# A fixed expert with 64 places, the lightest with 32, and small products moved inside a large one

## The reference

```
lg  = (xt @ w_rg).astype(float32) + b_rg;  grp = argmax(lg)      # one of 4 groups
le  = (xt @ w_re + b_re)[rows, grp]                              # its 4 experts
top_p, top_i = top_k(softmax(le), 2)                             # two experts a token
combine[token, expert] = softmax(lg)[grp] * top_p / sum(top_p)
for e in range(16):
    h = silu(xt @ w_gate[e]) * (xt @ w_up[e])                    # 1024 -> 512
    y = y + combine[:, e:e + 1] * (h @ w_down[e])                # 512 -> 1024
```

## Time and profile before

| | |
|---|---|
| median of 3 runs | 734.3 us (731.09 to 735.54) |
| profiled execution | 737.11 us, of which 735.4 us are its span |
| busy in the span | PE 691.0 us (94%), DVE 260.0, ACT 184.3, POOL 143.9 |
| DMA | 185.66 MB, mean 252 GB/s |
| start of the expert products | 447.6 us |
| last product of the last expert | ends at 717.0 us |

### The profile page before, as it was taken

The page is one execution under the profiler, slowest core; times in us unless marked ns, Lnnn a source line. Parts: engine busy times, 40 slices in busy tenths (PEclk is TensorE's granted clock), DMA queues, the critical chain, the costliest instruction groups (busy, mean ns, idle before and its releaser), DMA issues.

```text
span 735.4 us, 14789 instructions
## 1 busy us (share of the span) xinstructions
PE 691.0 (94%) x5461; PEld 443.2 (60%) x5461; DVE 260.0 (35%) x807; ACT 184.3 (25%) x459; POOL 143.9 (20%) x227
## 2 busy tenths in 40 slices
PE   4999999999997988998999999999999999999886
PEld 2476587848545464556555558965658675555442
DVE  4156310147344648754343653011121101111216
ACT  3110213112134864683332111000110010111104
POOL 0404007220242178300000201011111211111000
PEclk9999999999999899999999898999999999999999
DMA  9996138243578177403595248969999999999973
GB/s 343 369 317 206 46 130 285 64 166 115 191 239 320 35 197 197 148 1 117 209 423 210 73 172 303 391 219 391 360 396 408 385 369 383 367 365 394 378 286 131
DMA packets 56833, 185.66 MB, mean 252 GB/s; under 512 B 9182, under 2 KB 30975, under 8 KB 50738
## 3 DMA queue, kind: packets, MB, share of 16 engines
q1 hardware_dynamic: 44770, 152.54, 55.0%
q0 software_dynamic: 11984, 32.11, 14.3%
HBM read 172.97 MB, written 14.32 MB: 255 GB/s over the span
## 4 chain that ended last, share of the span: by engine, by line
PE 82%; DMA 8%; DVE 5%; ACT 3%; issue 1%; SPq 0%; DVEq 0%; ACTq 0%
PE ps L682 76%; DMA ring<-in_w_down_dram 6%; PE ps L929 2%; PE ps L1207 2%; DMA ring<-in_w_out_dram 1%; DMA ring<-in_w_in_dram 1%; PE ps L956 1%; PE ps L776 1%; ACT tabs L1595 1%; PE ps L832 0%; DVE tabs L1989 0%; DVE ugr L1965 0%; DVE vnr L2136 0%; DVE xr L2132 0%; PE ps L1074 0%
## 5 line engine op out<-in xcount | busy, mean ns | idle before, releaser
L682 PE MATMUL ps<-ring,xr 128*128 128x512 f32 (+3 forms) x640 | 138.8, 414 | 9.6 <-DMA ring<-in_w_in_dram 9.6
L682 PEld LDWEIGHTS ps<-ring,xr 128*128 128x128 f32 (+1 forms) x640 | 68.4, 151 | 72.2 <-issue 58.9
L682 PE MATMUL ps<-ring,work 128*32 128x128 f32 (+2 forms) x512 | 76.0, 381 | 2.2 <-DMA ring<-in_w_out_dram 1.6
L682 PE MATMUL ps<-ring,vnr 128*64 128x256 f32 (+1 forms) x1024 | 72.6, 328 | 0.0
L426 POOL DMA_DIRECT2D ring<-in_sel_pages_dram x96 | 51.5, 536 | 93.1 <-issue 57.0
L682 PEld LDWEIGHTS ps<-ring,vnr 128*64 128x64 f32 (+1 forms) x1024 | 49.4, 123 | 23.5 <-issue 6.6
L2464 DVE COPY vnr<-ps 128x256 f32<-128x256 f32 (+2 forms) x16 | 8.5, 533 | 150.8 <-PE ps L1207 150.8
L682 PE MATMUL ps<-ring,qT 128*32 128x256 f32 (+2 forms) x304 | 57.9, 506 | 3.3 <-DMA ring<-in_w_down_dram 2.6
L682 PE MATMUL ps<-ring 128*128 128x128 f32 (+1 forms) x512 | 59.6, 279 | 0.0
L2734 POOL DMA_INDIRECT x_rows<-kvn,qbd x14 | 20.7, 1480 | 198.6 <-DVE kvn L2510 67.2
L682 PEld LDWEIGHTS ps<-ring 128*128 128x128 f32 x512 | 58.8, 191 | 0.3 <-issue 0.2
(11 more groups left out here) (394 smaller groups left out, 830.3 us busy)
## 6 DMA issues: line engine op xcount, KB each, us to landing
ring<-in_w_gate_dram SPq DMA_DIRECT2D x11, 2048.0 KB, 20.4
ring<-in_w_up_dram SPq DMA_DIRECT2D x10, 2048.0 KB, 22.0
ring<-in_w_down_dram SPq DMA_DIRECT2D x10, 2048.0 KB, 26.1
xr<-in_w_gate_dram SPq DMA_DIRECT2D x5, 2048.0 KB, 24.2
tabs<-in_w_up_dram SPq DMA_DIRECT2D x5, 2048.0 KB, 26.4
ring<-in_cmp_pages_dram SPq DMA_DIRECT2D x64, 128.0 KB, 5.3
ring<-in_cmp_pages_dram POOLq DMA_DIRECT2D x64, 128.0 KB, 5.5
ring<-in_w_in_dram SPq DMA_DIRECT2D x3, 2048.0 KB, 9.3
```

What stands on the lines that cost most here:

```text
L682: return nc.tensor.matmul(out, lhsT, rhs, start=start, stop=stop)
```

## The change

Expert 0 gets 64 places instead of 128 and the light form of product, which the first place did not have before. Place 3 gets 32 places instead of 64 and now takes the lightest of the fourteen; it has a form of its own (`tiny_gate_up`, `tiny_turned`, `tiny_down`): four products side by side in quarters of the array. The other places keep their sizes.

The router products of the last two tiles and two of the table products run between the inner steps of the last output product, not ahead of it. The table of gate weights (`weights_in_slots`, and `placed_weights` on VectorE) is built behind the first expert's gate and up products; in its old place there are five products of `kept_warm` where there were four. Three of the four pieces of down 2 are issued ahead of gate 4, once the table of weights is there; only the fourth still waits for the second up product. VectorE's product of h for expert 1 now waits for expert 0's down product, since h of expert 0 lies in the same buffer. The last up load is issued in two halves, and the last up product starts on the first.

```
+TINY_CAP = 32
 FIXED = 2
-HEAVY = (E - FIXED) // 2
-FULL_AT = (6, 8)
-FULL = len(FULL_AT)
-PASSES = 1 + -(-(TOK - LIGHT_CAP) // CAP)
+CAPS = (64, 128, 96, 32, 96, 64, 128, 64, 128, 64, 96, 64, 96, 96, 64, 64)
+FULL, HEAVY, PLAIN = (sum(c >= least for c in CAPS[FIXED:]) for least in (CAP, MIDDLE_CAP, LIGHT_CAP))
+PASSES = 1 + -(-(TOK - TINY_CAP) // CAP)
...
+    by_size = np.argsort([-n for n in CAPS[FIXED:]], kind="stable")
+    c[:, C_SX + by_size] = np.arange(E - FIXED)
...
+        hT_tiny, sg_tiny, h_tiny = qf[:, 512:640], qf[:, 1536:1664], qf[:, 1792:1920]
...
-            return cap_of(n) == cap_of(n - 1)
+            return cap_of(n) == cap_of(n - 1) or {cap_of(n), cap_of(n - 1)} == {LIGHT_CAP, TINY_CAP}
...
+                if n == E - 1:
+                    load(up_slots[n % 3][:, 0:SLOT // 2], slab("w_up", e)[:, 0:SLOT // 2], "spare_in")
+                    load(up_slots[n % 3][:, SLOT // 2:SLOT], slab("w_up", e)[:, SLOT // 2:SLOT], "wu_in%d" % (n % 3))
+                    return
...
-                if n == FIXED:
-                    sp.wait_ge(sem("flag_ready"), 1)
-                    sp.wait_ge(sem("u_mm"), 2)
-                for f in range(FE):
+                for f in range(FE - 1 if n == FIXED else 0, FE):
+                    if n == FIXED:
+                        sp.wait_ge(sem("u_mm"), 2)
                     load(down_slots[2][f], slab("w_down", placed[n])[:, D * f:D * f + D], "wd_in2")
...
                     up_in_turn(placed[n], n)
+                    sp.wait_ge(sem("flag_ready"), 1)
+                    sp.wait_ge(sem("slots_ready"), 3)
+                    for f in range(FE - 1):
+                        load(down_slots[2][f], slab("w_down", placed[FIXED])[:, D * f:D * f + D], "wd_in2")
...
                     ins = mm(pb[4 + n][:, :], mixT[r % 2][:, k, :], wo[:, k, W * n:W * n + W], k == 0, k == KD - 1)
+                    if r == 4 and n == 1 and k == 1:
+                        router(2)
+                    elif r == 4 and n == 1 and k == 3:
+                        tokens_in_slots(0)
+                        tokens_in_slots(1)
+                    elif r == 4 and n == 1 and k == 5:
+                        router(3)
...
-            router(2)
-            tokens_in_slots(0)
-            tokens_in_slots(1)
-            router(3)
...
-            kept_warm(3)
+            kept_warm(5)
             te.wait_ge(sem("weights_ready"), 1)
-            weights_in_slots()
-            kept_warm(1)
...
-                if is_split(n - 1):
+                if n and is_split(n - 1):
                     te.wait_ge(sem("hl_ready"), split_before(n))
-                else:
+                elif n:
...
-                        up_in(n)
-                        weights = up_slots[n % 3]
+                        if n == E - 1:
+                            te.wait_ge(sem("spare_in"), 48)
+                        else:
+                            up_in(n)
+                        weights = up_slots[n % 3 if n else 1]
                     wv = weights.rearrange("p (k f) -> p k f", k=KD)
                     for k in range(KD):
+                        if n == E - 1 and bank == 3 and k == KD // 2:
+                            up_in(n)
                         for q in range(2):
...
+            def tiny_gate_up(n):
+
+                te.wait_ge(sem("xt_ready"), 2 * n + 2)
+                if is_split(n - 1):
+                    te.wait_ge(sem("hl_ready"), split_before(n))
+                else:
+                    te.wait_ge(sem("h_ready"), n)
+                for bank, done in ((2, "g_mm"), (3, "u_mm")):
+                    if bank == 2:
+                        te.wait_ge(sem("wg_in%d" % (n % 3)), 16 * (n // 3 + 1))
+                        weights = gate_slots[n % 3]
+                    else:
+                        up_in(n)
+                        weights = up_slots[n % 3]
+                    wv = weights.rearrange("p (k f) -> p k f", k=KD)
+                    for k in range(KD):
+                        for q in range(4):
+                            ins = mm(pb[bank][32 * q:32 * q + 32, 0:128], xeT[n % 2][:, k, 0:TINY_CAP],
+                                     wv[:, k, 128 * q:128 * q + 128], k == 0, k == KD - 1)
+                    ins.then_inc(sem(done), 1)
+
+            def tiny_turned(n):
+
+                te.wait_ge(sem("hl_ready"), split_before(n) + 1)
+                te.wait_ge(sem("y_out0"), n - 1)
+                te.wait_ge(sem("y_out1"), n - 1)
+                nc.tensor.transpose(pb[5 + 2 * (n % 2)][:, 0:P], h_tiny, ident).then_inc(sem("hl_turned"), 1)
+
+            def tiny_down(n):
+
+                te.wait_ge(sem("h_ready"), n + 1)
+                te.wait_ge(sem("wd_in%d" % (n % 3)), DOWN_LOADS[n % 3] * (n // 3 + 1))
+                wv = down_slots[n % 3]
+                for f in range(FE):
+                    for d in range(4):
+                        ins = mm(pb[4 + 2 * (n % 2)][32 * d:32 * d + TINY_CAP, 0:256], hT_tiny[:, 32 * f:32 * f + TINY_CAP],
+                                 wv[f][:, 256 * d:256 * d + 256], f == 0, f == FE - 1)
+                        if f == FE - 1 and d % 2:
+                            ins.then_inc(sem("y_mm"), 1)
+
             def turn_of(n):
 
...
             turn_of(1)
+            weights_in_slots()
+            light_turned(0)
             first_of(1)
...
+            def placed_weights():
+
                 dve.wait_ge(sem("slot_mm"), 2)
                 in_order(pb[7][:, 128:128 + E])
                 link(V.tensor_copy(slot_w[:, 0:FIXED], pb[7][:, 128:128 + FIXED]))
                 link(V.tensor_copy(slot_w[:, FIXED:E], in_place))
                 for q in range(4):
                     V.tensor_copy(slot_w_rest[32 * q:32 * q + 32, :], slot_w[64:96, 0:E])
+                    V.tensor_copy(slot_w_low[32 * q:32 * q + 32, :], slot_w[0:32, 0:E])
                 V.tensor_copy(slot_w_high[64:128, :], slot_w[0:64, 0:E]).then_inc(sem("slots_ready"), 1)
 
             def overflow_flag():
...
-                after(dve, "y_mm", 2 * n - 2)
+                after(dve, "y_mm", 2 if n == 1 else 2 * n - 2)
...
-                    dve.wait_ge(sem("slots_ready"), 3)
                 for n in range(E * b, E * b + E - 1):
                     rows_out(n + 1)
                     multiplied(n)
+                    if n == 0:
+                        placed_weights()
```

More of the change, by code:

```diff
@@ L61, with cap_of, is_tiny @@
 LIGHT_CAP = 64
+TINY_CAP = 32
 FIXED = 2
[L63 to L66 removed]
+CAPS = (64, 128, 96, 32, 96, 64, 128, 64, 128, 64, 96, 64, 96, 96, 64, 64)
+FULL, HEAVY, PLAIN = (sum(c >= least for c in CAPS[FIXED:]) for least in (CAP, MIDDLE_CAP, LIGHT_CAP))
+PASSES = 1 + -(-(TOK - TINY_CAP) // CAP)
 EPS = 1e-6
+def cap_of(n):
+    return CAPS[n] if n < E else CAP
 def is_light(n):
[L72 to L79 removed]
+    return cap_of(n) == LIGHT_CAP
+def is_tiny(n):
+    return cap_of(n) == TINY_CAP
 BIG = 1e30
@@ L162, in constants @@
     c[:, C_WB:C_WB + WIN] = np.where(dist <= WIN, slope[:, None] * dist, BIG)
-    at = np.arange(FIXED, E)
-    light = np.array([is_light(n) for n in at])
-    full = np.array([cap_of(n) == CAP for n in at])
-    middle = ~light & ~full
-    c[:, C_SX:C_SX + E - FIXED] = np.select([full, middle], [np.cumsum(full) - 1, FULL + np.cumsum(middle) - 1],
-                                            HEAVY + np.cumsum(light) - 1)
+    by_size = np.argsort([-n for n in CAPS[FIXED:]], kind="stable")
+    c[:, C_SX + by_size] = np.arange(E - FIXED)
     j = np.arange(SEQ)
@@ L1284, in light_turned @@
                 te.wait_ge(sem("hl_ready"), split_before(n) + 1)
-                te.wait_ge(sem("y_out0"), n - 1)
-                te.wait_ge(sem("y_out1"), n - 1)
+                after(te, "y_out0", n - 1)
+                after(te, "y_out1", n - 1)
                 for c in range(2):
@@ L1366, in first_of @@
             def first_of(n):
-                if is_light(n):
+                if is_tiny(n):
+                    tiny_gate_up(n)
+                elif is_light(n):
                     light_gate_up(n)
@@ L1375, in last_of @@
             def last_of(n):
-                if is_light(n):
+                if is_tiny(n):
+                    tiny_down(n)
+                elif is_light(n):
                     light_down(n)
@@ L1394, in _ @@
                 last_of(n - 1)
-                if is_light(n):
+                if is_tiny(n):
+                    tiny_turned(n)
+                elif is_light(n):
                     light_turned(n)
@@ L1780, in y_out @@
                 par = n % 2
+                if cap == TINY_CAP:
+                    for d in range(2):
+                        ins = A(ye[par][0:TINY_CAP, 256 * d:256 * d + 256], pb[4 + 2 * par][32 * d:32 * d + TINY_CAP, 0:256],
+                                ACT.Copy, scale=slot_w_low[32 * d:32 * d + TINY_CAP, n:n + 1])
+                    ins.then_inc(sem("y_out0"), 1)
+                    return
                 if cap == MIDDLE_CAP:
@@ L2434, in overflow_flag @@
```

(18 more changed lines are left out.)

18 lines of the change are left out of this document (11 added, 7 removed).

## The result

The changed kernel takes 724.69 us (median of 20 executions, 720.18 to 734.78) against 733.71 us for the kernel before (20 executions). The ratio is 0.9886, 95% interval 0.9864 to 0.9907: 8.4 us (6.8 to 10.0) or 1.1% faster by the ratio, 9.0 by the medians. The ratio is of fast runs alone: two of the twenty executions, of 732.0 and 734.8 us, were in the chip's slower state and count in the median only. The forecast was 725.8 us.

A forecast was written before the change was run, and what follows sets the result against it. The prediction took the stream of weight loads as the bound. Hole 7, front 1.3 and last up 0.2 sum to 8.5 us: 737.11 becomes 728.6 profiled, 725.8 against the median; the forecast's own range is 721 to 729.

The forecast's parts named there:

- What bounds: Mixture: the stream of weight loads sets the end; TensorE's savings after 500 us bring no load forward.
- The hole: Load stream, 480 to 500 us: 6.4 us without transfer close; stream comes forward 5.9 to 7.9, taken as 7.
- Gate 5's issue: SP's wait for gate 2's product: freed 6.7 us earlier, at 487.4, with 2.5 us to spare.
- The new wait: Ahead of gate 2: VectorE forms h of expert 1 only after down 0, costing 0.8 us.
- Gathers: POOL's gather for expert 5 lands at 521.1, TensorE wants it at about 521.9: it just fits.
- The front: Routing's end: mixed small products keep the clock, so the residual starts earlier; 1.4 us gained or 1.3 lost, taken as +1.3.
- The last up: Up 15 in halves: its product can end at 709.7, but hangs on the chain behind down 13; 0.2 us, at most 2.
- Place 3, early down 2, the moved table: Mixture's start: place 3 saves TensorE 3.4 and 1.8 us, not counted in the sum; SP's wait for the table costs nothing.
- In full: Rival, whole kernel: TensorE's time counts in full, 13.3 us gained, 721.0 us; chance 0.07.
- Given back: Rival: stream gains 5.9, front loses 1.3, half clock in the last chain takes 1.7; 2.9 us, 731.4; chance 0.22.
- Starved, at half clock: Rival, behind down 13's landing: TensorE waits for loads and runs at half clock to the end; 9.9 us slower, 744.2; chance 0.07.

The follow-up runs named there:

- place3_64: Changed kernel with 64 places at place 3 again instead of 32: 726.57 us, ratio 0.9900 to the kernel before.
- up_7_8: Changed kernel with the last eighth of the up loads of places 6 to 14 left out: 721.43 us, ratio 0.9839 to the kernel before.
- expert0_alone: Changed kernel with all undone but expert 0's 64 places and the later table of weights: 727.37 us, ratio 0.9916 to the kernel before.
- end_order: Changed kernel with sizes of places 3 and 13 swapped, expert 15's gate and up with their loads ahead of down 14: 724.70 us, ratio 0.9900.
- apart: Changed kernel with the router and table products again ahead of the last output product: 725.04 us, ratio 0.9894 to the kernel before.
- warm_mixed: Changed kernel with router(3) behind the last output product's fourth step, one warming product ahead of router(4) and one behind it: 723.42 us, ratio 0.9871.
- expert0_128: Changed kernel with expert 0 at 128 places in full form, its new wait gone, the weight table in its old place: 734.15 us, ratio 0.9997.

## Why the prediction was right

Its number was right within 1.1 us, and its main step with it; but smaller terms were off and cancelled, and that part is luck. Counted from the first transposes, the last up load landed 6.9 us earlier (256.3 us and not 263.1), its product ended 1.7 us closer behind it, and the tail was 0.3 shorter: the 8.9 us of the mixture stage. The forecast had 7 and 0.2 for these, and 1.3 for the front, which gave 0.2.

- **What bounds.** Right. The stream of loads, not TensorE, sets the end: place3_64 adds 5.1 us of products and costs nothing that can be told, up_7_8 takes loads away and gains 3 to 4 us. Not tried was the hole by itself: no run issues gate 5 late with TensorE's work as in the changed kernel.
- **The hole.** Forecast 7 (5.9 to 7.9). (Six loads at the 5.9 printed are 35.4 us and not 35.2; the rows give 5.87.) Up 3 to up 5 took 10.0 us less: the six loads went at 5.5 us each, faster than the 5.9 I had from two of them. Then 32 loads from up 5 (495.1) to the last half of up 15 (695.9) took 200.8 us, 6.28 each and not 6.20, 2.3 us back. Net 7.7, and 6.9 from the first transposes, as up 3 landed 0.8 us later behind them. The total was right because one rate was better than forecast and the other worse. Why the rate fell a little was not tried.
- **Gate 5's issue.** Forecast 6.7 us earlier than before. Taken from the first transposes it went from 49.2 to 37.4 us, 11.9 us. I had charged the half clock (1.95 of 3.9 us) to expert 0's products in both kernels; it did not lie there this time, and they took 7.13 us: 2 of the 5 us. The other 3 I had left out: expert 0's transposes and the wait behind them take 1.2 us and not 2.8, as they are of 64 rows and at full clock, and the 1.5 us that TensorE waited for VectorE ahead of expert 1's products are filled by the table of weights. The 2.5 us to spare were really 7.8 (issued at 477.05, the loads ahead of it landed by 484.8).
- **The new wait.** Forecast 0.8 us at gate 2, measured 1.12.
- **Gathers.** "It just fits" held for expert 5, whose rows landed 0.8 us before TensorE wanted them. Expert 6's came too late, and this short wait lies in the chain that ended last (PE in order, of the changed kernel):

```profile
522.32 1.09 PE L1216 MATMUL ps<-cst,ugr 128*128 128x128 f32 x8 [0.81 <-DMA ugr<-h_rows,qbd]
```

- **The front.** Forecast +1.3, measured 0.2 over that stage. The step that failed is "I take +1.3, as the long run of small products is broken up": the product did keep the clock in this execution (whether for the mixing is open, see expert0_alone) and `residual(4, 1)` did come 1.8 us earlier, limited by `chosen_of(3)` as forecast, but the half clock then fell on the products behind it.
- **The last up.** Forecast 0.2, at most 2. Measured 1.7: the end of the product follows the landing by 2.0 us (697.9 against 695.9) where it was 3.7. The mechanism was right, its cover was not: I let the chain behind down 13 decide, but with its half-clock stretch of 1.7 us gone from there, the load was the limit.
- **Place 3, early down 2, the moved table.** Costed at nothing each, and each undone alone makes no difference that can be told.
- **Rivals.** *In full* (721.0): refuted by place3_64. *Given back* (731.4): only its front part came. *Starved, at half clock*: TensorE does wait more, and one stretch of 3.4 us fell to half, on down 12 (7.22 us against 5.5 in the earlier trace rows). It cost nothing there, because the last up was late anyway. The Trainium skill (TensorE: Matmul & The Clock Gate, HAM oscillation) has every tile cold where its compute is shorter than the wait for its load. In the changed kernel that condition is not met: each of the waits, 0.3 to 2.9 us, is shorter than the product behind it, so "by that rule the 744 would come" was a wrong use of it, and its trace neither confirms nor refutes the rule. In end_order one wait is longer, 2.9 us ahead of half an up product of 1.95, and there the trace agrees. What the rows show is that such waits are followed by half clock only sometimes: after 2.1 us here, but not after 2.2 and 2.9; in apart and warm_mixed not after 2.4, 2.9 and 3.0; in end_order after each of 2.9, 3.1 and 4.2, in expert0_128 after 3.65.

## What to carry to other kernels

When a queue of loads stays full to the end, look for the last place where it was empty, and for what kept the next load from being issued there: faster products are worth about that hole (6.4 us here, and the last load landed 6.9 earlier). After that they only lengthen TensorE's waits, and the time behind the last load to land (here half a product instead of a whole) is the next thing to shorten. Compare stages between two common events and not spans, when executions of the same code differ by 5 us before the change is even reached.

## What was not expected of the hardware

Full clock in one product was followed by half clock in later ones. All fourteen traces have half clock somewhere between the start of `out_product(4, 0)` and the end of expert 0's gate and up products; in eleven it is one stretch, of 6.8 or 10.2 us, and only its place differs. What decides the place was not found. And place3_64 ran at half clock for 20.5 us there, from about 423 us; its gather was 5 us later, and its mixture stage was no longer than the others'.
